# A hybrid encoder layer with 32 experts on one core: order of the expert products, gathers three pairs ahead, and a held-back third pair

## The chip, the cores and the metric

The kernel runs on one core of a Trainium2 chip. The metric is the time of one execution on the device in microseconds (us). Three runs of the kernel before gave 605.27, 605.85 and 606.26 us; the median is 605.85 us. One further execution was recorded by the profiler.

The engines are named as in the profile: PE is TensorE (PEld its weight load), DVE VectorE, ACT ScalarE, POOL GpSimd, SP SyncE. A q behind a name is the engine's own instruction queue, where it waits and issues transfers. 16 DMA engines serve the core; SyncE's transfers go through queue q1, ScalarE's through q10, GpSimd's indirect transfers through q0.

## The reference, cut to what matters

The layer normalises x, mixes tokens by attention and pooling, and then applies a mixture of experts to 768 tokens of width 1024. Only the last part and what leads to it are touched here.

```
h = x + token_mixer(rms_norm(x, g_attn_norm))
x = h + hier_moe(rms_norm(h, g_ffn_norm))

# hier_moe: softmax over 4 groups, best group; softmax over its 8 experts, best two; gate weights
for e in range(32):
    hdn = silu(x @ w_gate[e]) * (x @ w_up[e])        # (768, 1024) @ (1024, 256)
    y   = y + combine[:, e:e+1] * (hdn @ w_down[e])  # (768, 256) @ (256, 1024)
```

The kernel computes only the tokens that an expert was chosen for. Everything is float32 here; the weights of the 32 experts are 96 MB and are read once.

## The kernel before, in words

**Stages.** Up to about 270 us come projections, attention and pooling. Then, for six tiles of 128 tokens, the output product, the residual (h) and routing follow. Each tile of h is stored twice: into the output (SyncE, `store_h`) and into the scratch table token_rows (ScalarE, `store_row`). Routing gives every token a place in the list of each of its two experts. These lists are made by small one-hot products on TensorE (`slots`, `more_slots`): a column per expert, a row per place. Places 0 to 63 go to `idx_all`, with factors in `gate_all`; places 64 to 127, the first overflow, go to `idx_more` and `more_all`. Lists longer than that are read from the DRAM table slot_tokens, which GpSimd fills by scatters (`fill_slots`). ScalarE stores a table of gate factors (`store_gates`), each row waiting for GpSimd's `gate_row` and for the store before it.

**Pairs.** The experts are worked in 16 pairs. A pair is experts j and 16 + j, each with 64 rows: one in partitions 0 to 63, the other in 64 to 127 (lanes 0 and 1). For each pair GpSimd gathers 128 rows of h from token_rows; TensorE transposes them (line 858); ScalarE and VectorE copy them, scaled, to xT (1152, 1515); TensorE forms the gate products and the up products (871); ScalarE applies silu (1158), VectorE multiplies (1526); TensorE transposes the hidden rows (878), VectorE copies (1533); TensorE forms the down products (887, and 899 for the last pair, in halves); ScalarE and VectorE copy y (1163, 1538); GpSimd adds the rows into the output in DRAM by an indirect transfer that accumulates (1689; 1695 for the halves of the last pair). Additions are in order: each waits until the one before has landed.

**Overflow.** Where an expert of the pair has more than 64 tokens, the same weights are used a second time on other rows (`over` and its own semaphores). `first_pass` runs its opening (transposes, gate and up) right after the main gate and up products of the same pair; `rest_passes` runs its closing (down) after the main down product. The trace shows two such passes, one of them in pair 0.

**Weights.** Three buffers hold three pairs. Each pair is six transfers of 1 MB: gate, up and down for two lanes (`part_in[0..5]`). SyncE issues a transfer when the one three before it has landed, so three are under way (`load_pair`, line 279). From pair 3 on `refill` waits first (line 474) until the old contents are used: gate weights until gate products of pair j - 3 (with overflow) are done, then up, then down. Pair 2's transfers stand after the last `store_h`: four at once in the chain, then a wait for the first gather's rows, then two more.

**Order in a pair.** On TensorE: gate and up of pair j; opening of overflow j; transposes of pair j + 1; hidden transposes of j; down of j; closing of overflow j. GpSimd: gather for pair j + 2; overflow gather for j + 1 if j has none; addition of y of j.

Of the kernel before, what the change touches and what calls it, by code (L numbers as in the profile page):

```python
# [16 lines left out]
P = 128  # L17
# [76 lines left out]
def build(nc, a, out):  # L94
# [6 lines left out]
    with ctx:  # L101
# [3 lines left out]
        def region(size, *groups, pick):  # L105

            got = []
            for group in groups:
# [20 lines left out]
             ("idx_all", [P, PAIRS + 1], I32), ("idx_more", [P, PAIRS], I32), ("idx_now", [P, 7], I32), ("idx_last", [P, 2], I32),  # L129
# [117 lines left out]
        refill_go, dma_go = sem("refill_go"), sem("dma_go")  # L247
# [10 lines left out]
        GU_BANK = (2, 6)  # L258
        units = [(s, hp, qt) for hp in range(2) for s in range(2) for qt in range(TILES[s])]
# [36 lines left out]
        def passes_counter(eng):  # L296
# [5 lines left out]
            def first(j, opening):  # L302
                todo = eng.value_load(counts_i[0:1, 3, bass.ds(j, 1)], min_val=0, max_val=PASSES - 1)
                with eng.If(todo > 0):
                    opening(eng.snap(before))
                return todo
# [9 lines left out]
            return first, rest  # L316
# [43 lines left out]
        def _(sp):  # L360
# [94 lines left out]

            def load_last_down(j, b):

                src = a["w_down"][0].rearrange("(l j) (p k) (n f) -> j n p l k f", l=2, k=2, n=2)
                for n in range(2):
                    sp.wait_ge(part_in[1 + n], 16 * (j + 1))  # L460
                    for lane in range(2):
                        dst = weights[b][:, lane, 2, :].rearrange("p (k n f) -> p n k f", k=2, n=2)
                        sp.dma_start(dst[:, n], src[j, n, :, lane]).then_inc(part_in[4 + n], 16)

            def refill(j, b):
# [5 lines left out]
                def used(kind):  # L471
                    sp.wait_ge(kind(main), j - 2)
                    sp.wait_ge(kind(over), passes)
                    sp.sem_inc(refill_go, 1)

                used(lambda q: q.g_mm)
                load_pair(sp, j, b, range(2))
                used(lambda q: q.gu_mm)
                load_pair(sp, j, b, range(2, 4))
                used(lambda q: q.y_mm)  # L480
                if isinstance(j, int):
                    load_last_down(j, b)
                else:
                    load_pair(sp, j, b, range(4, 6))

            with sp.Fori(1, PAIRS // 3) as i:
                for b in range(3):
                    refill(3 * i + b, b)
            refill(PAIRS - 1, 0)


        @block.tensor
        def _(pe):
# [285 lines left out]
            def slot_product(i, at, block, cols, last):  # L779

                for c in range(2):
                    mm = pe.matmul(ps[:, 5, at + cols.start * E:at + cols.stop * E], slot_a[:, i % SLOT_BUFS, 2 * block + c, :],
                                   slot_b[:, i % SLOT_BUFS, c, cols, :].rearrange("t n e -> t (n e)"),
                                   start=(i == 0 and block == 0 and c == 0), stop=(last and c == 1), skip_group_check=True)
                return mm

            def slots(i):
# [3 lines left out]
                slot_product(i, 0, 0, slice(0, 3), False).then_inc(slot_mm, 1)  # L791

            def last_slots():

                pe.wait_ge(slot_a_done, 2 * NT - 1)
                pe.wait_ge(slot_b_done, 2 * NT - 1)
                slot_product(NT - 1, 0, 0, slice(0, 1), False).then_inc(slot_mm, 1)
                pe.wait_ge(idx_done, 2)
                pe.wait_ge(slot_b_done, 2 * NT)
                slot_product(NT - 1, 0, 0, slice(1, 3), True).then_inc(slot_mm, 1)  # L800

            def more_slots(i):

                pe.wait_ge(slot_a_done, 2 * (i + 1))
                slot_product(i, 128, 1, slice(0, 3), i == NT - 1).then_inc(more_mm, 1)

            def keep_clock(n):

                for _ in range(n):
                    pe.matmul(ps[:, 3, 0:P], ones_bf, ltri_bf, start=True, stop=True)  # L810

            for i in range(NT):
# [10 lines left out]
                if i == NT - 1:  # L823
                    slots(0)
                    more_slots(0)
# [6 lines left out]
            ranks(last - 1)  # L832
            slots(2)
            slots(3)
            logits(last, 1)
            slots(last - 1)
            for i in range(1, last - 1):
                more_slots(i)
            pe.wait_ge(h_done, 2 * NT)
            keep_clock(8)  # L840
            ranks(last)
            last_slots()
            pe.wait_ge(pos_done, NT)
            pe.matmul(ps[:, 6, 128:128 + E], ones_bf, m_sum[:, 0, :], start=True, stop=True).then_inc(total_mm, 1)
            pe.wait_ge(idx_done, 5)
            more_slots(last - 1)
            more_slots(last)
# [13 lines left out]
            def gate_up(q, b, n):  # L861
                pe.wait_ge(q.x_act, n + 1)
                pe.wait_ge(q.x_dve, n + 1)
                for g in range(2):
                    if q is main:
                        for lane in range(2):
                            pe.wait_ge(part_in[2 * g + lane], 16 * (n + 1))
                    for k in range(KD):
                        for lane in range(2):
                            r = slice(lane * LANE, (lane + 1) * LANE)  # L870
                            mm = pe.matmul(ps[r, GU_BANK[q.o], g * FH:(g + 1) * FH], xT[:, q.o, k, r], w_gu(b, lane, k, g),  # L871
                                           start=(k == 0), stop=(k == KD - 1))
                    mm.then_inc((q.g_mm, q.gu_mm)[g], 1)
# [17 lines left out]
            def down_halves(b, n):  # L891

                pe.wait_ge(main.hT_done, n + 1)
                for half in range(2):
                    pe.wait_ge(part_in[4 + half], 16 * (n + 2))
# [919 lines left out]
```

## Time and profile before

| | |
|---|---|
| median of three runs | 605.85 us |
| profiled execution, in all | 604.86 us |
| its span, first to last instruction | 603.1 us |
| mean granted TensorE clock | 0.980 |
| PE busy | 529.3 us (88%) |
| DVE, ACT, POOL busy | 218.8, 169.5, 138.8 us |
| moved by DMA | 140.83 MB, mean 233 GB/s |
| SyncE's queue q1 | 124.33 MB |

The span is what the profile divides; the execution takes 1.8 us more. Busy time of PE includes modelled ends of pipelined products, so a busy PE is not always at work. The DMA share is the mean busy share of the 16 DMA engines in a stretch; it can come out slightly above 1. "Landing" is the time from the start of an issue to the semaphore's last increment.

### The profile page before, as it was taken

What the parts mean: (1) busy time and instruction counts of PE and PEld (TensorE: products, weight loads), DVE (VectorE), ACT (ScalarE), POOL (GpSimd) and SP (SyncE); (2) the same over time, 40 slices, a digit from 0 to 9 for tenths busy, and PEclk for the clock granted to TensorE, in tenths of its full rate; (3) what the DMA queues carried; (4) which work ended last, traced back from release to release, by engine and by line L of the source; (5) the groups of instructions that cost most, each with busy time, mean ns of one, the idle gap of its engine ahead of it and who ended that gap; (6) DMA issues with size and microseconds to landing.
All of it is one profiled execution on the core that took longest, in us unless ns stands there. A gap on an engine that the chain in (4) does not pass through costs nothing.

```text
span 603.1 us, 9578 instructions
## 1 busy us (share of the span) xinstructions
PE 529.3 (88%) x3304; PEld 390.6 (65%) x3305; DVE 218.8 (36%) x602; ACT 169.5 (28%) x421; POOL 138.8 (23%) x230
## 2 busy tenths in 40 slices
PE   5899999999989999999967888699988799897864
PEld 4888988987657677788866645366645456554431
DVE  4753243242667755427772111111121111211011
ACT  6833333332534333125432201111121011211010
POOL 0132232222513300004536022212202222222212
PEclk9999999999999999999998999899999979999898
DMA  8741000012323111199978499999999999999994
GB/s 323 293 113 37 3 33 1 2 68 77 106 71 96 44 36 36 35 344 420 409 254 316 152 326 386 364 381 383 365 385 384 418 393 378 356 363 369 357 342 120
DMA packets 33447, 140.83 MB, mean 233 GB/s; under 512 B 10488, under 2 KB 11147, under 8 KB 21350
## 3 DMA queue, kind: packets, MB, share of 16 engines
q1 hardware_dynamic: 25776, 124.33, 53.5%
q0 software_dynamic: 5856, 12.60, 8.7%
q10 hardware_dynamic: 1766, 3.25, 1.4%
q8 instruction: 29, 0.48, 0.3%
q14 instruction: 20, 0.16, 0.1%
HBM read 131.15 MB, written 16.46 MB: 245 GB/s over the span
## 4 chain that ended last, share of the span: by engine, by line
DMA 42%; PE 11%; issue 1%; DVE 1%; ACT 1%; POOL 0%; ACTq 0%; SPq 0%; DVEq 0%; POOLq 0%
DMA expert_w<-in_w_gate 19%; DMA expert_w<-in_w_up 19%; DMA token_gates<-gate_rows 4%; PE ps L871 4%; PE ps L508 1%; PE ps L509 1%; PE ps L513 1%; PE ps L887 1%; PE ps L767 1%; PE ps L756 1%; POOL out L1695 0%; PE ps L899 0%; DVE hid L1526 0%; ACT s_act L1158 0%; DVE h_sb L1371 0%
## 5 line engine op out<-in xcount | busy, mean ns | idle before, releaser
L871 PE MATMUL ps<-expert_w,xT 128*64 128x256 f32 x1152 | 130.4, 383 | 18.2 <-DMA expert_w<-in_w_gate 6.0
L871 PEld LDWEIGHTS ps<-expert_w,xT 128*64 128x64 f32 x1152 | 96.9, 138 | 55.3 <-issue 19.4
L887 PE MATMUL ps<-expert_w,hT 128*64 128x512 f32 x272 | 66.0, 628 | 20.6 <-DVE hT L1533 14.8
L1689 POOL DMA_INDIRECT out<-y_sb,idx_now x17 | 27.2, 1597 | 161.6 <-issue 121.5
L1526 DVE SCALAR_TENSOR_TENSOR hid<-s_act,gate,ps 128x256 f32<-128x256 f32 x18 | 12.0, 666 | 141.1 <-ACT s_act L1158 141.1
L887 PEld LDWEIGHTS ps<-expert_w,hT 128*64 128x64 f32 x272 | 22.5, 143 | 53.4 <-issue 48.4
L1158 ACT ACTIVATE s_act<-ps,gate 128x256 f32<-128x256 f32 x18 | 8.5, 474 | 132.6 <-PE ps L871 132.6
L508 PE MATMUL ps<-w_in_hi,aT_hi 128*128 128x384 f32 (+2 forms) x120 | 43.7, 369 | 0.0
L509 PE MATMUL ps<-w_in_lo,aT_hi 128*128 128x384 f32 (+2 forms) x120 | 40.8, 345 | 0.0
L1538 DVE COPY y_sb<-ps 128x512 f32<-128x512 f32 x18 | 12.5, 692 | 77.3 <-PE ps L887 72.9
L1163 ACT ACTIVATE y_sb<-ps 128x512 f32<-128x512 f32 x18 | 10.8, 597 | 81.8 <-PE ps L887 77.9
L1061 ACT ACTIVATE p_sb<-ps,a_stat 128x512 f32<-128x512 f32 (+1 forms) x24 | 14.8, 616 | 54.5 <-DVE a_stat L1342 54.2
L1152 ACT ACTIVATE xT<-ps,g_x 128x128 f32<-128x128 f32 x72 | 20.6, 368 | 15.3 <-PE ps L858 15.3
L513 PE MATMUL ps<-w_in_hi,aT_lo 128*128 128x384 f32 (+2 forms) x120 | 24.3, 344 | 0.0
L509 PEld LDWEIGHTS ps<-w_in_lo,aT_hi 128*128 128x128 f32 x120 | 22.6, 188 | 2.7 <-issue 1.2
L508 PEld LDWEIGHTS ps<-w_in_hi,aT_hi 128*128 128x128 f32 x120 | 22.6, 188 | 2.7 <-issue 1.2
L858 PE MATMUL ps<-consts_sb,g_rows 128*128 128x128 f32 x128 | 19.0, 293 | 4.2 <-DMA g_rows<-token_rows,idx_now 4.2
L858 PEld LDWEIGHTS ps<-consts_sb,g_rows 128*128 128x128 f32 x128 | 15.8, 195 | 10.1 <-DMA g_rows<-token_rows,idx_now 5.1
L513 PEld LDWEIGHTS ps<-w_in_hi,aT_lo 128*128 128x128 f32 x120 | 20.6, 188 | 1.6
L614 PE MATMUL ps<-w_ukv_sb,cT_kv 128*128 128x512 f32 x48 | 21.6, 592 | 0.0
L508 PE MATMUL ps<-w_out_hi_o,o_hi 128*128 128x512 f32 x48 | 19.8, 413 | 1.0 <-DVE route_f L1364 1.0
L706 PEld LDWEIGHTS ps<-pT,v_sb 128*128 128x128 f32 x160 | 19.7, 191 | 0.9
(227 smaller groups left out, 932.4 us busy)
## 6 DMA issues: line engine op xcount, KB each, us to landing
expert_w<-in_w_gate SPq DMA_DIRECT2D x32, 1024.0 KB, 9.5
expert_w<-in_w_up SPq DMA_DIRECT2D x32, 1024.0 KB, 9.4
expert_w<-in_w_down SPq DMA_DIRECT2D x30, 1024.0 KB, 9.8
w_in_raw<-in_w_in SPq DMA_DIRECT2D x8, 608.0 KB, 9.9
w_out_raw<-in_w_out SPq DMA_DIRECT2D x8, 512.0 KB, 3.9
token_rows<-h_sb ACTq DMA_DIRECT2D x6, 512.0 KB, 8.4
out<-h_sb SPq DMA_DIRECT2D x6, 512.0 KB, 10.5
x_sb<-in_x_prompt SPq DMA_DIRECT2D x4, 512.0 KB, 11.6
```

What stands on the lines that cost most here:

```text
L508: pe.matmul(dst, l_hi(k), r_hi(k), start=(first and k == ks[0]), stop=False)
L509: pe.matmul(dst, l_hi(k), r_lo(k), start=False, stop=False)
L513: mm = pe.matmul(dst, l_lo(k), r_hi(k), start=False, stop=(last and k == ks[-1]))
L614: mm = pe.matmul(ps[:, 5 + n, :], cT_kv[:, k, :], w_ukv[:, k, n * 512:(n + 1) * 512], start=(k == 0), stop=(k == KKV - 1))
L706: mm = pe.matmul(ps[:, 6, at:at + P], v_sb[:, FIRST[s] + c, h * DV:(h + 1) * DV], pT[:, m % 2, u, c, :], start=(c == 0), stop=(c == TILES[ ...
L858: mm = pe.transpose(ps[:, banks + k // 4, (k % 4) * P:(k % 4 + 1) * P], blocks[:, k, :], ident)
L871: mm = pe.matmul(ps[r, GU_BANK[q.o], g * FH:(g + 1) * FH], xT[:, q.o, k, r], w_gu(b, lane, k, g), start=(k == 0), stop=(k == KD - 1))
L887: mm = pe.matmul(ps[r, 4 + half, :], hT[:, q.o, k, r], w_dn(b, lane, k, half), start=(k == 0), stop=(k == 1))
L1061: act.activation(p_sb[:, w % 4, 0:n], ps[:, 2 * (m % 2) + u, 0:n], ACT.Exp, bias=a_stat[:, w % 4, 1:2], scale=SCALE, accum_out=a_stat[:, w ...
L1152: ins = act.activation(xT[:, q.o, k, :], ps[:, bank, k * P:(k + 1) * P], ACT.Copy, scale=g_x[:, k:k + 1])
L1538: dve.tensor_copy(y_sb[:, buf, 512:1024], ps[:, 5, :]).then_inc(q.y_dve, 1)
L1689: pool.indirect_dma_start(out=out, out_offset=bass.IndirectOffsetOnAxis(ap=idx, axis=0), in_=y_sb[:, buf, :], in_offset=None, compute_op=A ...
```

## The change

1. TensorE's order in a pair becomes: transposes of pair j + 1; hidden transposes of j; gate and up of pair j + 1; down of j; closing of overflow j; opening of overflow j + 1. Before the loop stand gate of pair 0, transposes of its overflow rows, up of pair 0, gate and up of its overflow. ScalarE and VectorE follow the same order.
2. `refill(j)` issues gate j, up j and then the down weights of pair j - 1 (after the down products of pair j - 4). Chains of three transfers under way stay.
3. GpSimd gathers for pair j + 3, not j + 2. Ahead of the loop it gathers pair 0, pair 1, the first overflow rows of pair 0 (without looking whether there are any, signal `first_more_in`) and pair 2, and only then runs `gate_row` of the last tile.
4. The overflow lists are formed in a PSUM bank of their own (3), before the factors, and some small products move.
5. Pair 2's transfers: two (gate) at once, then the wait for the first gather's rows, then four.

```diff
@@ SyncE
-            load_pair(sp, 2, 2, range(4))
+            load_pair(sp, 2, 2, range(2))
             sp.wait_ge(main.gathered[0], 16)
-            load_pair(sp, 2, 2, range(4, 6))
+            load_pair(sp, 2, 2, range(2, 6))
...
+            def refill(j, b, first=False):
+                earlier = sp.snap(more)
                 todo = sp.value_load(counts_i[0:1, 3, bass.ds(j - 3, 1)], min_val=0, max_val=PASSES - 1)
                 sp.reg_add(more, more, todo)
                 passes = sp.snap(more)
+                used(main.g_mm, j - 2, over.g_mm, passes)
+                sp.wait_ge(part_in[3], 16 * j)
+                load_part(0, j, b)
+                sp.wait_ge(part_in[4], 16 * (j - 1))
+                load_part(1, j, b)
+                used(main.gu_mm, j - 2, over.gu_mm, passes)
+                sp.wait_ge(part_in[5], 16 * (j - 1))
+                load_part(2, j, b)
+                sp.wait_ge(part_in[0], 16 * (j + 1))
+                load_part(3, j, b)
+                if not first:
+                    used(main.y_mm, j - 3, over.y_mm, earlier)
+                    sp.wait_ge(part_in[1], 16 * (j + 1))
+                    load_part(4, j - 1, (b + 2) % 3)
+                    sp.wait_ge(part_in[2], 16 * (j + 1))
+                    load_part(5, j - 1, (b + 2) % 3)
...
             refill(PAIRS - 1, 0)
+            used(main.y_mm, PAIRS - 3, over.y_mm, sp.snap(more))
+            load_last_down(PAIRS - 1, 0)
@@ TensorE
             def pair(j, i, b, last):
-                gate_up(main, b, j)
-                ...
-                todo = first_pass(j, opening)
+                nb = (b + 1) % 3
+                if not last:
+                    gather_transposes(main, g_rows[:, nb, :], main.gathered[nb], i + 1 if b < 2 else i + 2)
+                hidden_transposes(main, j)
+                if not last:
+                    gate_up(main, nb, j + 1)
...
                     down(main, b, j)
-                rest_passes(todo, closing, again)
+                rest_passes(overflow(j), closing, again)
+                if not last:
+                    first_pass(overflow(j + 1), opening)
 
             gather_transposes(main, g_rows[:, 0, :], main.gathered[0], 1)
+            x_ready(main, 0)
+            gate_or_up(main, 0, 0, 0)
+            todo = overflow(0)
+            first_pass(todo, lambda n: gather_transposes(over, more_rows[:, :], first_more_in, 1))
+            gate_or_up(main, 0, 0, 1)
+            first_pass(todo, lambda n: gate_up(over, 0, 0))
+            pe.wait_ge(idx_done, 13)
             run_pairs(pe, pair)
@@ GpSimd
-                    if not (isinstance(j, int) and j == 0):
-                        pool.wait_ge(main.x_tr, j)
-                    gather_pair(j + 2, (b + 2) % 3, 2 * j + 1)
+                    pool.wait_ge(main.x_tr, j + 1)
+                    gather_pair(j + 3, b, 2 * j + 1)
...
             gather(g_rows[:, 1, :], table, idx_all[:, 1:2], main.gathered[1])
+            pool.wait_ge(idx_done, 4)
+            gather(more_rows[:, :], table, idx_more[:, 0:1], first_more_in)
+            gather(g_rows[:, 2, :], table, idx_all[:, 2:3], main.gathered[2])
             gate_row(NT - 1)
```

## Rows read from the trace of the kernel before

**Rows 1.** The stretches view: start:end, length, busy by engine, PEclk, DMA share, GB/s.

```profile
370.00:430.00 60.00, 50.38 (x366) 32.91 (x363) 10.12 (x21) 9.06 (x25) 13.57 (x19) 0.97 1.02 377
```

**Rows 2.** SyncE's waits from 340 us (last line: 365 to 385): us, times, longest.

```profile
SPq L279 <- DMA expert_w<-in_w_down: 61.2, 24, 4.4
SPq L474 <- PE ps L871: 20.1, 4, 14.1
SPq L474 <- PE ps L887: 10.6, 2, 8.4
...
SPq L474 <- PE ps L887: 2.2, 1, 2.2
```

**Rows 3.** DMA view, 370 to 430 us: packets, MB, share; issues, us to landing.

```profile
q1 hardware_dynamic: 2540, 18.49, 76.5%
q0 software_dynamic: 1298, 3.92, 24.1%
...
out<-y_sb,idx_now POOLq DMA_INDIRECT x4, 10.4
g_rows<-token_rows,idx_now POOLq DMA_INDIRECT x4, 11.9
```

**Rows 4.** The stretches view again, the two holes.

```profile
335.00:340.00 5.00, 3.59 (x35) 2.89 (x36) 0.86 (x2) 1.14 (x4) 1.44 (x3) 1.00 0.29 68
...
350.00:355.00 5.00, 3.65 (x16) 1.26 (x16) 1.05 (x3) 0.64 (x2) 1.63 (x1) 1.00 0.88 261
```

**Rows 5.** Instructions by time, 315 to 341 us: start, us, what [idle before].

```profile
315.31 0.50 DVE L1472 TENSOR_SCALAR idx_all<-ps,consts_sb 64x16 int32<-64x16 f32 x2 [0.33 <-PE ps L782]
...
318.03 1.15 POOL L1670 DMA_INDIRECT g_rows<-token_rows,idx_all  x1 [5.98 <-issue]
...
319.48 0.99 POOL L1670 DMA_INDIRECT g_rows<-token_rows,idx_all  x1 [0.30 <-issue]
...
322.17 0.22 POOL L1642 TENSOR_TENSOR gate_rows<-route_f 128x16 f32<-128x16 f32 x1
...
326.82 7.13 PE L871 MATMUL ps<-expert_w,xT 128*64 128x256 f32 x64 [1.71 <-ACT xT L1152]
...
333.88 1.17 PE L858 MATMUL ps<-consts_sb,more_rows 128*128 128x128 f32 x8
...
336.46 7.13 PE L871 MATMUL ps<-expert_w,xT 128*64 128x256 f32 x64 [1.41 <-DVE xT L1515]
...
340.48 2.16 SPq L279 DMA_DIRECT2D expert_w<-in_w_gate  x2
```

**Rows 6.** The chain of waits that ended last: start, us, what.

```profile
307.10 12.40 DMA token_gates<-gate_rows
...
319.58 4.23 DMA token_gates<-gate_rows
```

**Rows 7.** DMA issues of 306 to 307 us: KB, us to landing.

```profile
token_rows<-h_sb ACTq DMA_DIRECT2D x1, 512.0 KB, 10.3
```

**Rows 8.** Instructions by time, the tail.

```profile
576.35 3.65 PE L887 MATMUL ps<-expert_w,hT 128*64 128x512 f32 x16 [2.30 <-DMA expert_w<-in_w_down]
...
581.87 1.60 POOL L1689 DMA_INDIRECT out<-y_sb,idx_now  x1 [12.75 <-issue]
...
586.53 3.67 PE L871 MATMUL ps<-expert_w,xT 128*64 128x256 f32 x32 [1.48 <-DMA expert_w<-in_w_up]
...
596.05 1.55 POOL L1695 DMA_INDIRECT out<-y_sb,idx_last  x1 [12.58 <-ACT y_sb L1163]
```

**Rows 9.** Landing of additions issued at 351, 358, 581 and 596 us.

```profile
out<-y_sb,idx_now POOLq DMA_INDIRECT x1, 6.3
...
out<-y_sb,idx_now POOLq DMA_INDIRECT x1, 7.8
...
out<-y_sb,idx_now POOLq DMA_INDIRECT x1, 10.5
...
out<-y_sb,idx_last POOLq DMA_INDIRECT x1, 4.3
```

More of the change, by code:

```diff
@@ L315, in rest @@
                             eng.reg_add(before, before, 1)
-            return first, rest
+            return overflow, first, rest
         def y_free(eng, q, n):
@@ L454, in _, with load_part @@
             sp.reg_mov(more, 0)
+            def load_part(n, j, b):
+                what, lane = n // 2, n % 2
+                k = 2 if what == 2 else KD
+                src = a[("w_gate", "w_up", "w_down")[what]][0, bass.ds(PAIRS * lane + j, 1)].rearrange("e (p k) f -> p (e k f)", k=k)
+                sp.dma_start(weights[b][:, lane, what, :], src).then_inc(part_in[n], 16)
             def load_last_down(j, b):
@@ L469, in refill @@
                 passes = sp.snap(more)
[L471 to L486, printed above, removed]
+                used(main.g_mm, j - 2, over.g_mm, passes)
[14 more added lines that the diff above has]
+                    load_part(5, j - 1, (b + 2) % 3)
+            for b in range(3):
+                refill(3 + b, b, b == 0)
+            with sp.Fori(2, PAIRS // 3) as i:
                 for b in range(3):
@@ L921, in again @@
                 def again(n):
-                    opening(n)
+                    more_transposes()
+                    gate_up(over, b, n)
                     closing(n)
-                todo = first_pass(j, opening)
-                if not last:
-                    nb = (b + 1) % 3
-                    gather_transposes(main, g_rows[:, nb, :], main.gathered[nb], i + 1 if b < 2 else i + 2)
-                hidden_transposes(main, j)
                 if last:
@@ L1562, in pair @@
                 hT_copy(main, j)
+                if not last:
+                    hidden(main, j + 1, nb)
                 y_copy(main, j, b, last)
-                rest_passes(todo, closing, again)
+                rest_passes(overflow(j), closing, again)
+                if not last:
+                    first_pass(overflow(j + 1), opening)
             gates(0, 0)
             x_copy(main, 0)
+            hidden(main, 0, 0)
+            first_pass(overflow(0), opening)
             run_pairs(dve, pair)
@@ L1713, in more_gather, with first_more_place, first_more_gate @@
                 pool.tensor_copy(gate[:, 3:4, :], more_gate[:, bass.ds(j, 1), :]).then_inc(over.gate_done, 1)
+            def first_more_place(j):
+                pool.tensor_copy(idx_now[:, 6:7], idx_more[:, bass.ds(j, 1)]).then_inc(more_set, 1)
+            def first_more_gate(j):
+                pool.tensor_copy(gate[:, 3:4, :], more_all[:, bass.ds(j, 1), :]).then_inc(over.gate_done, 1)
             def first_more_gather(j):
@@ L1724, in first_more_gather @@
                     gather(more_rows[:, :], table, idx_now[:, 6:7], over.gathered[0])
-                    pool.tensor_copy(gate[:, 3:4, :], more_all[:, bass.ds(j, 1), :]).then_inc(over.gate_done, 1)
+                    first_more_gate(j)
             def more_add(j, n):
@@ L1781, in _ @@
             pool.wait_ge(idx_done, 9)
-            first_more_gather(0)
+            todo = pool.value_load(counts_i[0:1, 3, 0:1], min_val=0, max_val=PASSES - 1)
+            with pool.If(todo > 0):
+                first_more_place(0)
+                first_more_gate(0)
+                pool.reg_add(firsts, firsts, 1)
             fill_slots(NT - 2)
```

187 lines of the change are left out of this document (104 added, 83 removed).

## The prediction

> **What bounds the kernel now.** I read the page's DMA line first, then busy time by stretch. From about 340 us the 16 DMA engines are full: share 1.02 over 370 to 430 us, with TensorE's granted clock at 0.97 of full speed [rows 1]. The reader is to see next who holds up the queue that issues the expert weights. SyncE waited 61.2 us for down weights alone, as long for gate weights, and 30.7 us (20.1 and 10.6) for TensorE. Those are six waits, the last of them 2.2 us between 365 and 385 us [rows 2]; after it there is none. So from there on the pace is the DMA's: TensorE needs 7.13 us for gate and up products, 3.65 for down and 1.17 for transposes [rows 5, 8], 12 us and a few short waits, in a pair whose 6.29 MB of weights take 20 us (18.49 MB in 60 us [rows 3]). A new order of products cannot shorten that. It can only change three things: when the full stretch begins, how many bytes and holes are in it, and what follows it.
>
> **Prices.** Weights took 76.5% of 60 us for 18.49 MB, 0.403 MB/us, so a 2.10 MB kind of weights (two lanes) costs 5.2 us of engine time. Gathers and additions took 24.1% of 60 us, 14.5 us; nine were issued in that stretch (four gathers, one of overflow rows and four additions) [rows 3], so 1.6 us each. In 335 to 340 us the engines are nearly idle (0.29); in 350 to 355 there is a second, small hole (0.88) [rows 4].
>
> **Front: until the first gate product.** It starts at 326.82 us [rows 5]. The chain behind it is ScalarE's stores of gates: the fifth store landed 12.40 us after its issue, the sixth waited for it and for another 4.23 us, then came the function table load and x copies [rows 6]. GpSimd's first gather started at 318.03 although the list of tokens was ready at 315.81 [rows 5]; token_rows, issued at 306.68, landed 10.3 us later, at 317.0 [rows 7]. GpSimd starts a gather about 1 us after its last wait ends, so this is what it waited for.
> The change holds back the third pair's last four weight transfers. Two up transfers, 2.1 MB, no longer compete with token_rows. From 306.5 us some 3 MB remain (h store 0.5, gate 2.1, rows 0.5); at the 390 to 425 GB/s of that stretch I estimate they are through by 315. Then the token list binds: 315.81 plus 1 us, plus 0.2 for four more slot products ahead of the last router products, so the first gather starts at 317.0, 1.0 earlier. But two more gathers are put ahead of gate_row. Each costs 1.45 us of GpSimd (318.03 to 319.48), so gate_row ends at 317.0 + 4 x 1.45 + 1.4 = 324.2 (before 322.39 [rows 5]) and ScalarE's last store moves from 323.88 to about 324.3. I take +0.4 us for the first gate product. Bounds: -1.5 (both chains free) to +2.9 (nothing gained from the hold, two gathers in full). If the first gather stays at 318.03 but the rest is as above, gate_row ends at 325.2 and the first product moves by +1.5; that is rival D.
> The Trainium skill (DMA: Bandwidth & Descriptors, Queues, rings and completion order) says each DMA engine takes turns between the queues with work, a packet at a time. By that the depth of SyncE's queue would not slow ScalarE's, the hold would bring no earlier gather, and rival D would be the case. The trace leans against it: 0.5 MB on ScalarE's queue took 10.3 us [rows 7].
> The order of the last slot products costs nothing more: VectorE's chain to the counts ends at 320.5, and the transposes wait for TensorE's clock-keeping products, about 324, in both kernels. These transposes (1.1 us) are done before ScalarE is ready.
>
> **Overflow of pair 0.** Between the end of the first products and the start of the overflow products lie 2.58 us (333.88 to 336.46), transposes of 1.17 and then copies of x [rows 5]. Now the transposes stand between gate and up products, and the copies (1.41) run under the up product, half of 7.13 us: 2.58 becomes 1.17, -1.4. The overflow rows are asked for at about 320; even at the 10.5 us of rows 9 they land before 331, when they are wanted. SyncE's first refill waits for the overflow gate product: 340.48 + 0.4 - 1.4 = 339.5, **-1.0 us** for the start of the full stretch. Held-back weights (4.2 MB, 10.4 us of engines) and gathers lie between 321 and 336, in the old hole, and cost nothing; their user, gate product 2, comes at about 365.
>
> **The second hole.** It is there because the fourth pair's down weights waited 8.4 us for down products [rows 2]. Now gate and up of the next pair are issued first. By TensorE's durations the second pair's gate product ends at 349.1, its up at 352.7, and down 0 with its overflow at 361.5. Gate 3, up 3, gate 4 and up 4 (4 x 5.2 us from 341.5) keep the engines full to 362.3, with addition 0 to 364. Down 3 is asked for at 361.6, so no hole: 0.12 x 5 us, **-0.7 us**. Slack 2 to 3 us; without it the old hole returns further back.
>
> **Gathers three ahead.** Gathers 0 to 3 now lie before the full stretch, instead of 0 to 2: **-1.6 us**. Gathers 16 and 17 read only out-of-range indices. GpSimd starts each after x_tr of its own pair, one pair later in count; nobody waits, since rows are wanted three pairs on. Bounds 0 (gather 3 comes late, GpSimd's first pair waits for the slot stores) to -1.8.
>
> **The tail.** This is where I expect loss. Before, the last down weights landed at about 594.7, 8.2 us after the last up weights (586.4), with addition 14 among them (issued 581.87 [rows 8]). Then half 0's addition went out at 596.05 and the span ended at 603.1, 7.05 us later. In the new order down 14 is transferred after up 15, and down product 14 stands behind gate and up 15 on TensorE. Up 15 lands at 586.4 - 1.0 - 0.7 - 1.6 - 5.2 = 577.9, down 14 at 583.1; its product 3.65, copy 0.7, and 1.05 to GpSimd's start (as 580.82 to 581.87) give addition 14 at 588.65. Half 0 waits for that addition to land, which goes out 6.8 us later than before although all weights are in at 589.7 (583.1 and 8.2 less addition 14's 1.6). End = 588.65 + L + 1.0 + 7.05 = 596.7 + L, L being the landing time of addition 14.
> Rows for L: 4.3 us for half rows with idle engines, 6.3 and 7.8 for whole rows as the engines refill, 10.5 beside full weights [rows 9]. Addition 14 starts moving as the weights end; I take 5.3, midway between 4.3 and 6.3. End of span 602.0 against 603.1: **-1.1 us**. The profiled execution took 604.86 in all; the median of the runs is 605.85, 1.0 above it. So 604.7.
>
> **Rivals.**
> A, the tail's wait is cheap and the front gains: L of 4.5 and the first product 1 us earlier than I take it: 605.85 - 2.9 = 603.0. For it: the engines are empty when addition 14 moves, and four serial gathers are the only thing that delays ScalarE. Against: whole rows never landed in under 6.3 in this trace.
> B, nothing gained where it counts: rows 1's pace drifts by a percent (2 us over 220), or gather 3 is late and a hole of 2 us opens where down 3 waits for the overflow's down products; 605.85 within 1: about 605.8. For it: SyncE waits mostly for transfers, not for TensorE [rows 2]. Against: the two idle patches of rows 4 are real and their causes are removed.
> C, slower: the last two additions queue behind addition 14. It decides from L = 7.6 on (596.7 + L over 603.1 + 1.2) and at 10.5 the end is 607.2, +4.1. For it: every addition beside full traffic took over 10 us and addition 14 is issued while the last 1 us of down weights still moves. Against: 6.3 already in a half idle stretch. At L of 8.5 the time is 605.85 + 2.1 = 607.9.
> D, the hold does not free the gathers: the first product at +1.5 instead of +0.4, 604.7 + 1.1 = 605.8, no change that can be told. For it: with gate weights of 2.1 MB still ahead the same queue is just as busy until 315. Against: then token_rows must stay as slow as in rows 7 with 2 MB less to compete.
> D is what the Trainium skill's rule of turns (DMA: Bandwidth & Descriptors, Queues, rings and completion order) leads to.
>
> **How the numbers follow.** A change of this kernel can be told from 0.2%, 1.2 us. My forecast 604.7 lies at that edge: I give it 0.38, own range 603.6 to 605.4, half of it counted faster; A 0.24, all faster; B 0.13, of which 0.03 at its worse end is slower; D 0.07, same; C 0.18, slower. That makes faster 0.43, same 0.19 + 0.10 + 0.07 = 0.36, slower 0.21. The range 601.9 to 607.4 takes A with 1 us of room and C up to L of about 8; the remainder of C and of the best front case is outside.
>
> **What would show it.** Gather 0 at 317.0 and four gathers in a row; ScalarE's last store of gates near 324.3; first refill at 339.5; the engines at share 1.0 from 341.5 through 355 and no wait for down products that empties them; the last up weights near 578; addition 14 near 588.7, and half 0's addition held by its landing, not by ScalarE's copy. Wrong would be: gates later than 328; a hole after 360; L over 7; or a pace in the full stretch other than about 19.3 us a pair (first gate weights of pair 5 asked for at 375.5, of pair 15 at 568.6).

## The result: 3% slower

| | before | after |
|---|---|---|
| median, run side by side | 606.06 us | 627.45 us (4 runs, 622.16 to 632.66) |
| ratio, 95% interval | | 1.0315 (1.026 to 1.0369) |
| profiled execution, its span | 604.86, 603.1 us | 628.03, 626.4 us |
| mean granted TensorE clock | 0.980 | 0.952 |
| first gate product starts | 326.82 us | 330.61 us |
| from there to the end of the span | 276.3 us | 295.8 us |

One run of the kernel after (632.66 us) was in a slower state, and the ratio is formed without it.

The last two rows part the loss. The first gate product started anywhere from 326.15 to 331.44 us in executions of kernels with the same front (e1 and n5 below), so profiles are compared from that product on: 19.5 us are lost there.

The stretches view of the kernel after, as in [rows 1, 4] (start:end, length, busy of PE, PEld, DVE, ACT and POOL, PEclk, DMA share, GB/s):

```profile
340.00:345.00 5.00, 2.50 (x22) 1.54 (x18) 1.35 (x2) 1.62 (x5) 1.46 (x3) 0.94 0.49 180
345.00:350.00 5.00, 5.00 (x36) 3.80 (x34) 0.00 (x0) 0.00 (x0) 0.00 (x0) 0.72 0.33 89
360.00:365.00 5.00, 5.00 (x32) 2.04 (x28) 0.74 (x2) 0.55 (x2) 0.00 (x0) 1.00 0.59 200
370.00:430.00 60.00, 41.98 (x270) 24.36 (x270) 8.26 (x16) 7.24 (x19) 9.32 (x13) 0.86 0.92 341
430.00:490.00 60.00, 48.69 (x352) 30.36 (x354) 9.32 (x18) 8.27 (x23) 11.49 (x16) 0.94 0.93 353
```

The DMA engines are no longer full: their share is 0.92 from 370 to 430 us, where [rows 1] has 1.02, and 0.93 in the 60 us after. Two holes lie before that, one of them 10 us wide. TensorE's clock fell to 0.86, and it was busy for 41.98 of 60 us instead of 50.38. Who waits for whom, SyncE first (us, times, longest), then TensorE, both from 340 us on:

```profile
SPq L477 <- PE ps L894: 58.3, 12, 13.9
SPq L463 <- DMA expert_w<-in_w_up: 52.7, 21, 4.6
...
SPq L477 <- PE ps L919: 6.6, 4, 3.0
```

```profile
PE ps L884 <- issue: 21.2, 6, 7.3
PE ps L894 <- ACT xT L1199: 9.2, 8, 1.9
PE ps L894 <- DVE xT L1565: 8.4, 4, 2.5
PE ps L894 <- DMA expert_w<-in_w_gate: 7.0, 4, 2.3
```

SyncE's 30.7 us for TensorE [rows 2] became 64.9. TensorE in turn waits 17.6 us for copies of x, and 21.2 us for "issue": for nothing that the profile shows. The worst place, on TensorE's timeline (idle time and its releaser in brackets):

```profile
377.28 1.97 PE L884 MATMUL ps<-consts_sb,g_rows 128*128 128x128 f32 x8 [7.31 <-issue]
379.04 0.63 PE L910 MATMUL ps<-consts_sb,hid 128*128 128x128 f32 x2
380.48 9.51 PE L894 MATMUL ps<-expert_w,xT 128*64 128x256 f32 x64 [0.81 <-ACT xT L1199]
```

These transposes read the rows of pair 2, which GpSimd had asked for at 324.74 us. After the stall they take 1.97 instead of 1.17 us and the 64 products 9.51 instead of 7.13: TensorE stands at half clock (1.2 GHz) for part of them.

### The profile page after: what moved, and what is told of

Its sections match the earlier page's. It is cut to its first block, busy times and chain, and to the rows that moved or that the text cites. A ratio compares the mean times of both kernels' runs of the same rounds, so it can differ in the third digit from the quotient of the medians.

```text
span 626.4 us, 9737 instructions
## 1 busy us (share of the span) xinstructions
PE 539.0 (86%) x3308; PEld 394.9 (63%) x3309; DVE 219.4 (35%) x602; ACT 169.5 (27%) x421; POOL 140.2 (22%) x231
## 4 chain that ended last, share of the span: by engine, by line
DMA 25%; PE 23%; issue 5%; ACT 2%; POOL 1%; DVE 1%; DVEq 0%; POOLq 0%; ACTq 0%; SPq 0%
PE ps L894 13%; DMA expert_w<-in_w_gate 9%; DMA expert_w<-in_w_down 8%; PE ps L919 4%; DMA token_rows<-h_sb 2%; DMA more_rows<-token_rows,idx_now 2%; DMA token_gates<-gate_rows 2%; PE ps L884 1%; ACT xT L1199 1%; DMA out<-y_sb,idx_now 1%; PE ps L528 1%; PE ps L529 1%; PE ps L533 1%; PE ps L787 1%; DVE y_sb L1588 1%
## 5 line engine op out<-in xcount | busy, mean ns | idle before, releaser
L894 PE MATMUL ps<-expert_w,xT 128*64 128x256 f32 x1152 | 142.5, 410 | 28.6 <-ACT xT L1199 11.2
L919 PE MATMUL ps<-expert_w,hT 128*64 128x512 f32 x272 | 61.6, 593 | 2.4 <-DVE hT L1583 2.4
L884 PE MATMUL ps<-consts_sb,g_rows 128*128 128x128 f32 x128 | 20.7, 311 | 21.2 <-issue 21.2
L884 PEld LDWEIGHTS ps<-consts_sb,g_rows 128*128 128x128 f32 x128 | 17.1, 198 | 32.9 <-issue 32.9
L1565 DVE TENSOR_TENSOR xT<-ps,g_x 128x512 f32<-128x512 f32 x18 | 12.4, 691 | 24.7 <-PE ps L884 24.1
L648 PE MATMUL ps<-kT,qT 128*128 128x512 f32 (+1 forms) x48 | 20.8, 559 | 0.0
```

What stands on the lines that cost most here:

```text
L648: pe.matmul(ps[:, bank + u, 0:n], qT[:, h, q], kT[:, h, keys], start=True, stop=False)
L884: mm = pe.transpose(ps[:, banks + k // 4, (k % 4) * P:(k % 4 + 1) * P], blocks[:, k, :], ident)
L919: mm = pe.matmul(ps[r, 4 + half, :], hT[:, q.o, k, r], w_dn(b, lane, k, half), start=(k == 0), stop=(k == 1))
```

## Experiments

"Part" is the time from the first gate product to the end of the span in the one profiled execution (before: 276.3, after: 295.8). e1, n3, n5, n6 and n9 build on each other and lead from the new order as it was, 1.0315, down to 0.9942.

| run | what it is | us; the kernel before beside it | ratio (95%) | part |
|---|---|---|---|---|
| e1 | after, no further-pass loop on TensorE | 613.1, 607.57 | 1.0102 (1.0067 to 1.0137) | 283.0 |
| e2 | before, that loop's body twice | 678.96, 607.57 | 1.1203 (1.1125 to 1.1282) | 349.6 |
| e3 | new front and gathers, old order | 605.0, 607.57 | 0.9981 (0.9944 to 1.0017) | 275.9 |
| e4 | new order, front's timing undone | 625.76, 607.57 | 1.0326 (1.0254 to 1.0398) | 295.4 |
| n1 | before, no such loop | 605.66, 605.79 | 0.9985 (0.9956 to 1.0013) | 277.5 |
| n2 | e3, no such loop | 604.69, 605.79 | 0.9976 (0.9951 to 1.0001) | 274.7 |
| n3 | e1, overflow's x copied first | 608.65, 605.79 | 1.0047 (1.0022 to 1.0073) | 279.7 |
| n4 | n3, TensorE kept busy in gaps | 608.14, 605.79 | 1.0036 (1.001 to 1.0063) | 278.6 |
| n5 | n3, refill 4 waits like the others | 610.52, 607.73 | 1.005 (1.0022 to 1.0079) | 277.9 |
| n6 | n5, tail of the kernel before | 607.48, 607.73 | 1.001 (0.9977 to 1.0042) | 275.1 |
| n7 | n2, pair 0's overflow as in n3 | 603.59, 607.73 | 0.9948 (0.9922 to 0.9974) | 275.2 |
| n8 | n6, TensorE kept busy in gaps | 605.63, 607.73 | 0.9988 (0.9958 to 1.0019) | 272.2 |
| n9 | n6, x copied a pair ahead | 603.65, 606.55 | 0.9942 (0.9908 to 0.9976) | 271.5 |

**Code that never runs (e1, e2, n1).** A pair's code on TensorE holds, besides opening and closing, a loop over further passes (`again`) for lists over 128 tokens. With these inputs it never runs; kernels without it on TensorE leave that case out. That is e1 and all of n1 to n9.

```diff
@@ rest() in passes_counter: e1 (on after), n1 (on before)
+                    if eng.engine != nc.tensor.engine:
                       with eng.If(todo > 1):
                         with eng.Fori(1, todo) as p:
                             again(eng.snap(before))
@@ e2 (on before)
                             again(eng.snap(before))
+                            if eng.engine == nc.tensor.engine:
+                                again(eng.snap(before))
```

> The changed kernel with the never executed loop for a second and further overflow pass removed from TensorE's program (it is never entered with these inputs). Theory F (instruction supply): at the end of a pair without overflow TensorE now jumps over three blocks in a row (closing, further passes, opening of the next pair); the first time at each place it waits for instructions, 7.3, 4.9, 2.8, 2.8, 2.4 us ahead of the transposes of L884, and runs the next gate products at half clock. With the loop gone the jump is about half as long: idle time ahead of those transposes falls from 21 us to under 8, the time falls by 8 to 16 us, to about 614. Rival O (order): the new order itself makes TensorE late, the waits are something else: 627 within 3.

> The kernel before, with the never executed loop body of further overflow passes written twice in TensorE's program. Theory F: the jump at the end of a pair becomes as long as in the changed kernel, so TensorE waits for instructions ahead of the gate products of the first pairs, 2 to 7 us each in 3 to 5 places; a part of it is covered by the transfers, the time rises by 3 to 10 us, to 609 to 616. Rival O: no executed instruction has changed, 606 within 1.

> The kernel before, with the never executed loop for further overflow passes removed from TensorE's program. Theory F (16 KB blocks of instructions are fetched through the same DMA engines, and TensorE waits where it jumps into a block that is not there): 24 instead of 29 blocks on queue q8, the idle 4.0 us ahead of the gate products at 387 us goes away, but the transfers bound this stretch, so 0 to 1.5 us faster. If the code length costs time by itself, not by blocks: no fewer packets and 606 within 1.

The queue table has a kind that the prediction passed over, blocks of instructions (packets, MB, share). In this order e2, before and e1; after has 29 as before does, n1 has 24:

```profile
q8 instruction: 64, 1.05, 0.6%
```

```profile
q8 instruction: 29, 0.48, 0.3%
```

```profile
q8 instruction: 24, 0.39, 0.3%
```

A block is 16 KB and comes over the same 16 DMA engines as the weights. The seven copies of `again` hold five blocks (29 - 24). Without them the kernel after gets back 2.1 of its 3.2 points, and its "issue" waits ahead of the transposes fall from 21.2 to 8.1 us, both close to what was expected; the kernel before gains nothing that can be told (n1).

e2 missed its expectation by far: 71 us more, not 3 to 10. In e2 the code holds 34 blocks by these counts, and 64 come. I estimate from this 30 more in three further rounds of the loop, 10 a round, so its body is no longer held. TensorE waits 72.4 us for "issue" ahead of gate and up products, in 17 places. At the head of each of the four rounds it stands still for 8.2 to 10.5 us, here at the first:

```profile
401.52 8.61 PE L873 MATMUL ps<-expert_w,xT 128*64 128x256 f32 x64 [8.20 <-issue]
```

By the same estimate the body of before holds about 8 blocks (10 less 3 x 5/7), which stay. The Trainium skill (Runtime: NRT & Kernel Launch, Instruction fetch mechanics) gives TensorE 128 KiB in blocks of 16 KiB, which is eight, and says that a taken branch to a target outside the current two pages must wait for its block. The estimate fits the 128 KiB. It does not fit a window of two pages: in before none of the 29 blocks comes from 460 to 590 us, while the loop runs on. The measurement decides.

Before and after fetch the same number, and before stands still for its code too, once. This is TensorE at the gate product of pair 3 in before, then in n1, and between them the only block that comes from 383 to 388 us in before (it comes between 384 and 385):

```profile
387.11 8.81 PE L871 MATMUL ps<-expert_w,xT 128*64 128x256 f32 x64 [3.97 <-DMA expert_w<-in_w_gate]
```

```profile
q8 instruction: 1, 0.02, 6.0%
```

```profile
383.90 7.11 PE L872 MATMUL ps<-expert_w,xT 128*64 128x256 f32 x64
```

The row names gate weights as what ended the idle time, but both transfers of gate weights of pair 3 had landed by 350 us (issued at 340.48 and 341.03, landing after 5.2 and 8.4). In n1, without the five blocks, the gap is gone and the ratio stays, since there the DMA sets the pace: SyncE waits no more for TensorE after 385 us [rows 2]. In after there are six such waits, 21.2 us, in front of transposes of the next pair. There the jump leads over closing, `again` and opening in a row, where in before it leads over closing and `again`, and SyncE is waiting for TensorE already (58.3 us for gate and up products, up to 13.9 at a time). That the number and the place of the waits decide is inferred from e1 against n1; no run moved the jump alone. e1 and the runs built on it keep 8 to 9 us of "issue" waits.

**Front against order (e3, e4, n2).**

```diff
@@ e4 (on after)
-            load_pair(sp, 2, 2, range(2))
+            load_pair(sp, 2, 2, range(4))
             sp.wait_ge(main.gathered[0], 16)
-            load_pair(sp, 2, 2, range(2, 6))
+            load_pair(sp, 2, 2, range(4, 6))
...
             gather(g_rows[:, 1, :], table, idx_all[:, 1:2], main.gathered[1])
+            gate_row(NT - 1)
...
             gather(g_rows[:, 2, :], table, idx_all[:, 2:3], main.gathered[2])
-            gate_row(NT - 1)
@@ e3 (on after): pair(), refill() and the last down weights as in before; n2 is e3 with e1's edit
```

> The front and the gathers of the change alone: third pair held back, first overflow rows at once, overflow lists in their own bank, rows three pairs ahead. Order of the pair on TensorE, ScalarE, VectorE and the order of the weight transfers as in the kernel before. If the loss is all in the new order of the pair: equal to the kernel before or up to 2 us faster, 604 to 606, with no wait for instructions of over 4 us. Rival (the front costs): the first gate product is later and its refill too, 608 or more.

> The changed kernel with its front undone: four transfers of the third pair at once, and the first overflow rows and the third pair's rows gathered only behind the last gate row. Gathers stay three ahead. If the loss is in the order of the pair: 625 to 630, as the changed kernel. If the front causes a good part of it (half clock of the first products, late overflow): 620 or less.

> Front and gathers of the change with the old order of the pair, and the never executed loop removed from TensorE's program. Front alone gave a ratio of 0.998. Theory F: 24 blocks, the 4.8 us idle at 390 us gone, 0.99 to 0.998 of the kernel before. If the front's gain is noise and the blocks do not bind in the old order: 0.997 to 1.002.

The whole loss is the order's: e4 is as slow as after, e3 and n2 are within 0.3% of before. In the old order the jump over the same unused code costs nothing that can be told (e3 against n2). n2's median lies 1.0 us under n1's, and the intervals overlap: that, or nothing, is what gathers and hold bring.

**The overflow of pair 0 (n3).** ScalarE and VectorE, kernel after, 338 to 350 us, with TensorE's product that waits for them:

```profile
340.72 0.47 ACT L1205 ACTIVATE s_act<-ps,gate 128x256 f32<-128x256 f32 x1 [10.16 <-PE ps L894]
341.66 1.14 ACT L1199 ACTIVATE xT<-ps,g_x 128x128 f32<-128x128 f32 x4 [0.47 <-issue]
...
341.22 0.66 DVE L1576 SCALAR_TENSOR_TENSOR hid<-s_act,gate,ps 128x256 f32<-128x256 f32 x1 [11.87 <-ACT s_act L1205]
342.33 0.69 DVE L1565 TENSOR_TENSOR xT<-ps,g_x 128x512 f32<-128x512 f32 x1 [0.45 <-issue]
```

```profile
335.90 1.16 PE L884 MATMUL ps<-consts_sb,more_rows 128*128 128x128 f32 x8
337.00 3.67 PE L894 MATMUL ps<-expert_w,xT 128*64 128x256 f32 x32
343.17 7.09 PE L894 MATMUL ps<-expert_w,xT 128*64 128x256 f32 x48 [2.50 <-DVE xT L1565]
```

Transposes ended at 337.06 and both engines were idle, but their queues are in order: first silu and the hidden product of main 0, which need the up products (340.66), then the copies.

```diff
@@ n3 (on e1), ScalarE; VectorE alike with hidden()
             x_copy(main, 0)
+            todo = overflow(0)
+            first_pass(todo, lambda n: x_copy(over, n))
             silu(main, 0, 0)
-            first_pass(overflow(0), opening)
+            first_pass(todo, lambda n: silu(over, n, 3))
```

> The changed kernel without the never executed loop on TensorE, and with ScalarE and VectorE copying x of pair 0's overflow ahead of silu and product of its main pass, not behind. Theory Q (the 2.5 us ahead of the overflow's gate products are the copies queued behind the hidden rows of the main pass): that idle time falls to under 0.3 us, the products run at full clock (7.13 instead of 8.81), the first refill is 3 to 4 us earlier and the time falls from 613 by 2 to 5 us. Rival: the products wait for the overflow rows; nothing changes.

```profile
331.52 1.16 PE L885 MATMUL ps<-consts_sb,more_rows 128*128 128x128 f32 x8
332.61 10.58 PE L895 MATMUL ps<-expert_w,xT 128*64 128x256 f32 x96
```

Now 96 products run without a gap at full clock. SyncE's first refill goes out 11.9 us after the first gate product (339.84 less 327.92), against 18.0 in after and in e1, and the ratio falls from 1.0102 to 1.0047. Of the 6 us, 1.7 are not the edit's: the first 32 products ran at full clock in this execution (3.67 us) and not in after and e1 (5.36, 5.31). That comes and goes with the execution, since the first group is slow in e3 and n2 as well and at full clock in n5 and n6.

In the old order the same edit gives n7 0.9948 against n2 0.9976. The first refill of n7 is 1.5 us earlier after the first product than n2's, once n2's slow first group is taken out, as expected; but the intervals overlap and the parts are equal (275.2, 274.7), so a gain is not shown there.

**Half clock (n4, n8).**

```diff
@@ n4 (on n3); n8 the same on n6
                 hidden_transposes(main, j)
                 if not last:
+                    for _ in range(14):
+                        pe.matmul(ps[:, 2, 0:P], ones_bf, ltri_bf, start=True, stop=True)
                     gate_up(main, nb, j + 1)
```

> The same as the one with copies first, and 14 small bf16 products (128x128, about 1.1 us) on TensorE between the hidden transposes and the gate products of every pair, where it stood idle for 1 to 2.3 us. Theory C (half clock after idle gaps is a good part of the loss): gate and up products of all pairs take 7.1 us, none 8.7 or more, granted clock above 0.975, time 2 to 5 us less. Rival: the gap costs only its own length; the time is the same within 1 us.

> n6 with 14 small products into an unused bank between the hidden transposes and the gate products of each pair, which keep TensorE busy while x is copied. Theory (half clock after these gaps costs only where TensorE is late): main gate and up products 7.1 to 7.3 us instead of 8.5 to 9.9 and the time within 1.5 us of n6, as n4 was of n3. Rival (with holes and tail mended TensorE is now the bound): 2 us or more under n6.

Mean time of one gate or up product from 344 to 580 us: 406 ns in n3, 386 in n4 (first two numbers behind the bar: busy us, mean ns):

```profile
L895 PE MATMUL ps<-expert_w,xT 128*64 128x256 f32 x966 | 118.0, 406 | 27.0 <-DVE xT L1568 10.0 <-ACT xT L1200 8.0 <-DMA expert_w<-in_w_gate 7.0
```

```profile
L895 PE MATMUL ps<-expert_w,xT 128*64 128x256 f32 x985 | 112.5, 386 | 15.1 <-DVE xT L1570 6.9 <-ACT xT L1202 5.9 <-issue 2.3
```

So the slow groups are the clock: with TensorE kept busy one group in each run stays above 9 us (9.20 and 9.22), where n3 has five and n6 four. But both gains, 0.11 and 0.22 points, lie within the intervals (n8's median is 1.8 us under n6's, between its theory and its rival). The clock is not a cause that can be told, and it does not follow the time: n9, the fastest below, ran at a mean granted clock of 0.951, the kernel after at 0.952. Nor does the wait just ahead decide: in n3 a group took 8.81 us after 1.01 us of idle time and another 7.13 after 2.24.

**The hole at 350 to 360 us (n5).** `refill(3)` issues no down weights, so the first gate weights of pair 4 wait for the transfer just issued, not for the third before it.

```diff
@@ n5 (on n3), refill()
+                second = isinstance(j, int) and j == 4
-                sp.wait_ge(part_in[3], 16 * j)
+                sp.wait_ge(part_in[1 if second else 3], 16 * j)
...
```

> The kernel of n3 with one thing changed in SyncE's refills: gate and up weights of pair 4 wait for the third transfer issued before them (gate 3 lane 1, up 3 lane 0, up 3 lane 1), as all later ones do, not for the last one issued. Theory (the hole at 350 to 360 us, share 0.60 in n3, is this wait, which lets the queue run empty): SyncE issues the first gate weights of pair 4 near 351, not 355.4, the share of 350 to 360 is over 0.85, and the time falls by 2 to 4 us, ratio 0.999 to 1.001. Rival (the weights are early enough anyway and TensorE, with its stalls, sets the pace): the hole closes and the time stays, ratio 1.003 to 1.006. Rival (the hole is TensorE's lateness): the share stays under 0.7.

```profile
350.00:360.00 10.00, 8.93 (x56) 3.92 (x54) 1.79 (x3) 1.07 (x2) 1.64 (x1) 1.00 0.60 229
```

```profile
350.00:360.00 10.00, 9.96 (x76) 5.18 (x72) 1.03 (x2) 0.83 (x2) 0.00 (x0) 1.00 0.97 391
```

The hole (n3, then n5) closed as expected, the time did not move: the first rival. From 340 us on SyncE's waits for TensorE rose from 16.7 to 46.0 us. Weights that come earlier wait for buffers, so something else sets the end; n6 and n9 try the tail and TensorE's own waits.

**The tail (n6).** After, then n5, then n6 (GpSimd; addition 14, then half 0):

```profile
611.24 1.60 POOL L1742 DMA_INDIRECT out<-y_sb,idx_now  x1 [8.81 <-issue]
...
618.99 1.56 POOL L1748 DMA_INDIRECT out<-y_sb,idx_last  x1 [6.15 <-DMA out<-y_sb,idx_now]
620.85 1.56 POOL L1748 DMA_INDIRECT out<-y_sb,idx_last  x1 [0.30 <-issue]
```

```profile
594.83 1.60 POOL L1748 DMA_INDIRECT out<-y_sb,idx_now  x1 [9.34 <-issue]
602.05 1.56 POOL L1754 DMA_INDIRECT out<-y_sb,idx_last  x1 [5.63 <-DVE y_sb L1592]
```

```profile
587.93 1.60 POOL L1791 DMA_INDIRECT out<-y_sb,idx_now  x1 [5.03 <-DMA out<-y_sb,idx_now]
596.58 1.56 POOL L1797 DMA_INDIRECT out<-y_sb,idx_last  x1 [7.05 <-ACT y_sb L1248]
```

```diff
@@ n6 (on n5): order for pair 14 and 15 only
 SyncE    ... gate 14, up 14, down 13, down 14, gate 15, up 15, down 15
 TensorE  ... transposes 15, hidden 14, down 14, closing, gate and up 15, opening
 (pair 2 moves into the loop and pair 14 out of it; ScalarE and VectorE alike)
```

> n5 with the end of the kernel before: down weights 14 are transferred ahead of gate and up 15, and down product 14 with its copies stands ahead of gate and up 15 on TensorE. Pair 2 moves into the loop and pair 14 out of it, so that straight code and loop body keep their size. Theory (the new order loses in its tail, because addition 14 is issued when all weights have landed and both halves of 15 wait for its landing of over 6 us): addition 14 is issued some 8 us or more ahead of the last half, half 0 waits for ScalarE's copy of y, and the time is 3 to 5 us under n5's, ratio 0.991 to 0.996. Rival (the weights are the bound, the tail hides): the last weights land as in n5 and the end follows them by about 8.5 us as in the kernel before; within 1 us of n5.

In n5 addition 14 goes out 7.2 us before half 0 and holds it. The row names VectorE's copy of y (600.89 to 601.58), the last event ahead of it, but half 0 does not wait for that one: it waits for ScalarE's copy, done at 599.77, and for addition 14. In n6 addition 14 goes out 8.65 us before, and half 0 waits for ScalarE's copy, as in before. The profiled part shrank by 2.8 us, the ratio by 0.4 points (2.4 us). That is less than the 3 to 5 us expected and more than the rival's 1, and the intervals of n5 and n6 overlap: the mechanism is seen, and its price is not clear of noise.

**What is left of the new order (n7, n9).**

```diff
@@ n9 (on n6), TensorE; ScalarE and VectorE copy x of j + 2 behind silu and hidden of j + 1
-                if not last:
-                    gather_transposes(main, g_rows[:, nb, :], ...)
                 hidden_transposes(main, j)
                 if not last and not late:
                     gate_up(main, nb, j + 1)
+                    gather_transposes(main, g_rows[:, (b + 2) % 3, :], ...)
```

> The order of pairs, refills and tail of the kernel before, with the new front (gathers three ahead, third pair held back) and without TensorE's unused loop of further passes; in pair 0 alone the overflow's transposes stand between gate and up products, and ScalarE and VectorE copy its rows ahead of silu and the hidden product. Theory (the overflow step is worth what the prediction took, 1.4 us, when the copies are hidden, and the gathers 1.6 us, in the old order as well): overflow gate product 1.2 to 1.6 us earlier after the first product than in n2, first refill earlier by as much, ratio 0.992 to 0.997. Rival (a faster start of the full stretch is given back by turns of the DMA, as n2's and e3's gathers were): ratio 0.997 to 1.000.

> n6 with the transposes and copies of x moved one product earlier in the new order: gate and up j + 1, then the transposes of x for pair j + 2, then down j; ScalarE and VectorE copy x of j + 2 ahead of y of j, so that the copies lie under the down product. Nothing else of n6 is changed; instructions and bytes are the same. Theory (what is left of the new order's loss against the old one, n6 at 1.001 against n7 at 0.995, is that TensorE waits 1 to 2.7 us a pair for these copies, 20.7 us in n6, falls behind the weights, and SyncE waits 41.7 us for it): TensorE's wait for xT under 5 us from 340 us on, SyncE's wait for TensorE under 20 us, and the time 2 to 4 us under n6, ratio 0.993 to 0.997. Rival (SyncE's waits for TensorE only stand where else it would wait for transfers, and the loss is the issue order gate, up, down of the pair before): TensorE's waits go, the ratio stays between 0.999 and 1.003. Rival (y of j and so addition j and the down products behind it come later by the copies): SyncE's wait for down products grows over 10 us, ratio over 1.003.

TensorE's waits in n6, then in n9:

```profile
PE ps L926 <- ACT xT L1237: 12.2, 9, 1.8
PE ps L926 <- DVE xT L1609: 7.0, 3, 2.7
```

```profile
PE ps L926 <- ACT xT L1237: 2.2, 2, 1.2
```

The 19.2 us of waits for x became 2.2, though TensorE's waits for gathered rows rose from 3.6 to 10.2, and the ratio fell from 1.001 to 0.9942. The two intervals only just do not overlap. SyncE's waits for TensorE hardly fell, against what I expected: 42.4 us, after 46.0 in n6. That sum is a poor measure of the loss, since an early weight queue waits too. n7 and n9 are 0.5% and 0.6% faster than before; both intervals lie below 1, and they overlap almost wholly. So with all of this mended the new order is no better than the old one, and n7 changes less. Both leave out lists over 128 tokens: neither can replace the kernel before as it is, and no run has them with that loop. Beside n1, which also lacks it, n7's lead is 0.4 points.

## Why the prediction was wrong

**What bounds the kernel: the step that failed.** "TensorE needs ... 12 us and a few short waits, in a pair whose 6.29 MB of weights take 20 us. A new order of products cannot shorten that. It can only change three things." The step let the new order change nothing in TensorE's own time in a pair, and it put TensorE's new waits at nothing. They were not: 21.2 us, most of it for instruction blocks (worth 2.1 points of the ratio, about 13 us: e1), and 0.8 to 2.5 us for x in twelve places, 17.6 us in all (0.7 points, about 4 us: n9 against n6). The sum priced every instruction that is moved and none that is jumped over. [rows 5] already had the other half: 1.71 us of idle for x ahead of the first gate product and 1.41 ahead of the overflow's. In the old order only pair 0 and the overflow passes pay that, since transposes of j + 1 stood ahead of down j. The new order puts gate j + 1 right behind its own copies.

**Front.** Expected 0.4 us later. The last store into token_rows, ahead of all that this step prices, was issued 3.6 us later than before (310.29 against 306.68). Measured from it the first gate product came 0.2 us later: 20.3 us after it, before 20.1. The gathers came in a row, as expected (GpSimd's first and last row of the front):

```profile
320.66 1.15 POOL L1723 DMA_INDIRECT g_rows<-token_rows,idx_all  x1 [4.99 <-DVE idx_more L1520]
...
327.42 0.22 POOL L1695 TENSOR_TENSOR gate_rows<-route_f 128x16 f32<-128x16 f32 x1
```

By that 3.6 us the predicted 317.0 is 320.6, and gather 0 started at 320.66, 1.2 us after its list was ready (319.47). So the list held it and the size came out. But the hold is not shown to be what freed it. e4 issues pair 2's first four transfers ahead of the wait again, as before; there token_rows landed 8.2 us after its issue, against 8.9 in e3 with the hold, and gather 0 started 1.0 us after its list all the same. Rival D was right to doubt the hold and wrong about the gather's time. The good forecast of the front is in part luck.

**Overflow of pair 0.** Failed: "the copies (1.41) run under the up product". The copies stand behind silu and hidden of main 0 in their engines' queues. The first refill came at 348.63 instead of 339.5. Of these 9.1 us 3.4 are the later first product (330.61 against 327.2). The rest is, within 0.2 us, the idle 2.50 and both gate products at half clock, 1.7 each (5.36 against 3.67 for the first, 32 products each). Where the copies are hidden the step holds its size: from the first gate product to the end of the overflow products 16.77 us in [rows 5], 15.27 in n3 (327.92 to 343.19), 1.5 less.

**The second hole.** "So no hole" failed twice over. The first was at 340 to 350 us, from the late refill; the second (0.59 at 360 to 365) came from the wait in `refill(4)`, which the step did not read. Closing it alone was worth nothing that can be told (n5). So the 0.7 us was no gain either, and 0.12 x 5 us is 0.6.

**Gathers three ahead.** 1.6 us expected; hold and gathers together brought 1.0, within the intervals (n2 against n1).

**The tail.** The mechanism was right: in after half 0 waits for addition 14 to land. L, the landing time of addition 14 in the DMA view, was 6.8 us, and 6.3 in n5, against 5.3 taken and 7.6 as rival C's point. That alone would have moved the end by 1.5 us. But the sum placed down 14 by the weights' pace alone, and TensorE was later: addition 14 went out at 611.24, not 588.65. In n3 SyncE asked for the last gate weights 6.8 us earlier than in before, counted from the first gate product (234.9 against 241.7 us after it; the step took 8.5), and yet the end was 3.4 us later. n6 prices the new tail at about 2.4 us.

**Rivals.** None had TensorE as the bound. A and B fell with the main step. C had the sign right and the place wrong for most of it: the tail is about 0.4 of 3.2 points.

## What to carry to other kernels

Before moving code of a loop on an engine that is nearly a bound, read the instruction row of the queue table and ask what is jumped over, where, and whether anything covers the jump; code that never runs can cost time. When a consumer moves closer behind its producer, follow the in-order queue of every engine between them: a copy is hidden only if nothing that waits for something later stands ahead of it. Close a hole in the transfers only after asking who waits for those bytes: here the 10 us hole was free and waits of 1 to 2.7 us for copies were not. And do not trust the name beside an idle time: look up when what it names had landed.

## What the runs showed of the hardware

Instruction blocks of 16 KB travel over the DMA engines beside the data: 29 in before and after. TensorE stood still for up to 7.3 us while one of them came with those engines full (share 1.02 from 370 to 377 us in after). A loop body that is no longer held costs far more: five more blocks of unused branch made the kernel 12% slower, with 72.4 us of "issue" waits (e2). Four or five groups of gate and up products took 8.5 to 9.9 us instead of 7.13 (n3, n6, n9); with small products ahead one did (9.2 in n4 and in n8), at a gain of 0.1 to 0.2 points, inside the intervals. A 0.5 MB store landed in 8.2 us with three 1 MB transfers issued within 1 us of it on SyncE's queue (e4) and in 8.9 with two (e3). And a whole-row addition with the weights just through landed in 6.0 to 6.8 us (e1, after), nearer to the 6.3 of [rows 9] than to its 4.3 for half rows on idle engines.
